# Score matmuls of a recurrence step issued two groups at a time in the first token half

## The chip, the cores and the metric

The kernel runs on one core of a Trainium2 chip. The metric is the device time of one execution in microseconds (us); lower is better. The engines have their own in-order instruction queues and meet only through semaphores: PE (TensorE, the matrix engine), DVE (VectorE), ACT (ScalarE), POOL (GpSimd) and SP (SyncE, which here only issues transfers).

## What is computed

The reference is one layer of a decoder block over 2048 tokens of 1024 features. After a norm and a modulation, one large projection gives the columns of four token mixers and of their gates. The mixer that matters here is the gated linear recurrence, worked in chunks:

```python
h = rmsnorm(x, g_pre[l]) * (1.0 + scale[:, None]) + shift[:, None]
p = h @ w_in[l]                      # 1024 x 8704, split into mixers and gates
...
def step(S, inp):                    # gated recurrence, 4 heads of 64
    qc, kc, vc, gc = inp
    b = jnp.cumsum(gc, axis=2)
    o_inter = jnp.einsum('bhtk,bhkv->bhtv', qc * jnp.exp(b), S)
    decay = jnp.exp(jnp.where(causal, diff, NEG))      # diff = b_t - b_s
    scores = jnp.einsum('bhtk,bhtsk,bhsk->bhts', qc, decay, kc)
    o = o_inter + jnp.einsum('bhts,bhsv->bhtv', scores, vc)
    S_new = (jnp.exp(b_last[:, :, 0, :])[..., None] * S
             + jnp.einsum('bhsk,bhsv->bhkv', kc * jnp.exp(b_last - b), vc))
```

The other mixers are a multi-window pooling, a short convolution and a differential attention. All are gated, projected, merged and projected once more; a norm and the residual end the layer.

## The kernel before, in words

The program has two stages. The first (`trunk`) computes the projection and all mixers; the second (`merge_and_output`) merges. The change touches `trunk` alone.

**Products and slots.** The projection is a row of 476 products, 238 for each half of the tokens (1024 tokens each). A product is 12 matmuls of 128x512 (four weight blocks, three split parts each: lines 1790 to 1792) into one of two PSUM banks `gb`, in turn. Seven products j = 0 to 6 make one unit of two columns of tiles. Every engine walks through the same loop over slots n = 0, 1, 2, ...: in slot n PE does product n, and each engine adds, by a table of slots, the small work of the mixers. So the place of a piece of work is set by the slot in which it is written.

**What holds a product.** Product n needs its bank free (`bank_free`): the result of product n-2 must have been taken out. For j = 0, 2, 3, 6 ScalarE copies it (`copy_out`, line 1013), for j = 1, 4, 5 VectorE adds it to another (`add_out`, line 1324, called "the sum" below). Both are done at the head of slot n+1 of their engine for product n. Product n also needs its split weights, made three slots ahead by ScalarE (`high`, line 990) and VectorE (`low`, line 1314); VectorE's part waits for ScalarE's.

**The recurrence's steps.** There are 16 steps of 128 tokens, 8 in each half. In the first half step i has its base at slot 130 + 12i, in the second at 372 + 25i/2. "Slot +k" below is the slot k behind the base of its step. A step has four score groups r = 0 to 3 (`rounds`): each is 8 small matmuls of 64 rows (lines 1928 and 1931; the profile has two records for each, so 16) into PSUM tile `score[r % 2]`. VectorE takes each group out with four predicated copies (`pick`, lines 1535 and 1540) into `AT`. Group r may start when the copies of group r-2 are done. The first two groups belong to one half of the heads, the last two to the other.

In the first half, before the change, PE has the groups at slots +0, +2, +4, +6 and VectorE its copies at +1, +3, +5, +7. In the second half the groups stand two at a time, at +0 and +4, and the copies at +1, +2, +5, +6.

**What else VectorE has in those slots** (the steps overlap: work at a negative offset is of the step that follows). In slot +2: after the sum and the weight split, `shares` of the next step (lines 1480 and 1481, which wait for ScalarE's `B_k_s`, line 1135) and `finish` of the step before (lines 1568, 1570, 1573). In slot +3: `queries` (line 1484). In slot +4: `scan` (1488, 1492, 1494). In slots +5 and +6: `distances_x` (1504). In slot +7: `decay_keys` (1511). Within one slot the copies of `pick` come behind the sum and the weight split and ahead of the rest. On PE, slot +0 has the norm matmul of the step before (1958), +4 the transposes (1966, 1967), +8 the outputs (1945 to 1952), all behind the groups of their slot.

Of the kernel before, what the change touches and what calls it, by code (L numbers as in the profile page):

```python
# [107 lines left out]
def kind(u):  # L108
    col = column(u)
    if col >= MIX_TILES or col < LOCAL_TILES:  # L110
        return "plain"
    return {20: "q", 24: "k", 28: "v", 32: "gate"}[col - col % 4]
# [51 lines left out]
def trunk(nc, x, c, w_ada, b_ada, g_pre, g_post, w_in, consts, diff_lam, diff_norm, hgrn_lb, hgrn_norm, conv_w, pool_w, pool_scale,  # L164
# [7 lines left out]
    with ExitStack() as ctx:  # L172
# [241 lines left out]
        def finished(half, s, lag):  # L414

            return ending.get(piece(half, s, lag))
# [12 lines left out]
        def mix_step(slot, offset):  # L429

            return MIX_BASE.index(slot - offset) if slot - offset in MIX_BASE else None

        MIX_HALF = NT // 2

        def step_in(half, slot, offset):

            i = mix_step(slot, offset)
            return i if i is not None and i // MIX_HALF == half else None

        def score_step(n, r):  # L440

            i = step_in(0, n, 2 * r)
            return step_in(1, n, (0, 0, 4, 4)[r]) if i is None else i

        def pick_step(n, r):

            i = step_in(0, n, 2 * r + 1)
            return step_in(1, n, (1, 2, 5, 6)[r]) if i is None else i

        def later(ap, level):  # L450

            return ap.rearrange("p (n u) -> p n u", u=2 * LEVELS[level])[:, :, LEVELS[level]:]

        def later_packed(ap, level):

            return ap[:, 0:P // 2].rearrange("p (n u) -> p n u", u=LEVELS[level])
# [846 lines left out]
        def _(dve):  # L1303
# [225 lines left out]
            def pick(i, r):  # L1529
                dve.wait_ge(r_done, 4 * i + r + 1)  # L1530
                for y in range(4):
                    level = 4 * (r % 2) + y
                    if level < NL - 1:
                        m = LEVELS[level]
                        ins = nc.vector.copy_predicated(
                            AT[:, r // 2, :, :].rearrange("p h (n u) -> p h n u", u=2 * m)[:, :, :, m:],
                            later(masks[:, level, :], level).unsqueeze(1).to_broadcast([P, 2, P // (2 * m), m]),
                            score[r % 2][:, :, y, 0:P // 2].rearrange("p h (n u) -> p h n u", u=m))
                    else:
                        ins = nc.vector.copy_predicated(AT[:, r // 2, :, :], masks[:, level, :].unsqueeze(1).to_broadcast([P, 2, P]),  # L1540
                                                        score[r % 2][:, :, y, :])
                    if y < 3:
                        link(ins)
                ins.then_inc(picked, 1)
                dve.wait_ge(picked, 4 * i + r + 1)
# [87 lines left out]
            for n in range(SLOTS):  # L1633
# [17 lines left out]
                for b, off in OUT_SLOT.items():  # L1651
                    v, r = divmod(n - off, PER)
# [44 lines left out]
                for half, s in att_slot(n):  # L1697
# [7 lines left out]
                    i = finished(half, s, GATE) if half else None  # L1705
# [7 lines left out]
                    if n == MIX_BASE[MIX_HALF * half] - 16:  # L1713
                        begin_mixers(half)
                for r in range(4):
                    i = pick_step(n, r)
                    if i is not None:
                        pick(i, r)
                i = mix_step(n, -10)
                if i is not None:  # L1720
                    shares(i)
                i = mix_step(n, -9)
                if i is not None:
                    queries(i)
                i = mix_step(n, -8)
                if i is not None:
                    scan(i)
                i = mix_step(n, -7)
                if i is not None:
                    distances_x(i, 0, 0, 3)  # L1730
                i = mix_step(n, -6)
                if i is not None:
                    distances_x(i, 0, 3, NL - 1)
                i = mix_step(n, -5)
                if i is not None:
                    decay_keys(i)
                i = mix_step(n, -4)
                if i is not None:
                    decay_first_queries(i)
                i = mix_step(n, -3)  # L1740
# [3 lines left out]
                i = mix_step(n, -2)  # L1744
                if i is not None:
                    distances_x(i, 1, 2, NL - 1)
                i = mix_step(n, 11)
                if i is not None:
                    advance_state(i)
                i = mix_step(n, 12)  # L1750
                if i is not None:
                    pool_out(i)
                i = mix_step(n, 14)
                if i is not None:
                    finish(i)
                i = mix_step(n, 1)
# [4 lines left out]
        def _(pe):  # L1761
# [15 lines left out]
            def product(n, part):  # L1777
                u, j = divmod(n, PER)
                if part == 0:
                    if made(n):  # L1780
                        pe.wait_ge(wlo, made_before(n) + 1)
                    else:
                        pe.wait_ge(w_kept[n % RING], 16 * (ring_uses(n) + 1))
                    if u % NU == 0:
                        operand_ready(u // NU, j)
                    bank_free(n)
                to, fresh = gb[n % 2][:, :], j in (0, 1, 3)
                hi, lo = w_hi[n % RING], w_lo[n % RING]
                for k in range(part * KH // 2, (part + 1) * KH // 2):
                    mm(to, hi[:, k, :], h_hi[j][:, k, :], start=(fresh and k == 0), stop=False, skip_group_check=True)  # L1790
                    mm(to, hi[:, k, :], h_lo[j][:, k, :], start=False, stop=False, skip_group_check=True)  # L1791
                    last = mm(to, lo[:, k, :], h_hi[j][:, k, :], start=False, stop=(k == KH - 1), skip_group_check=True)  # L1792
                if part:
                    last.then_inc(product_done, 1)
# [98 lines left out]
            def attention_ahead(half, s):  # L1893
                z = piece(half, s)
                if z is not None:
                    scores(z)
                i = finished(half, s, GATE) if half else None
                if i is not None:
                    turn_back(i)

            def attention_behind(half, s):
                z = piece(half, s, VALUES)
                if z is not None:
                    values(z)
                z = piece(half, s, TURN)
                if z is not None:
                    turn(z)
                i = None if half else finished(half, s, ON)
                if i is not None:
                    turn_back(i)  # L1910

            def rounds(i, r):
                if r == 0:
                    pe.wait_ge(prep0, 2 * i + 2)
                if r == 1:
                    pe.wait_ge(q_ready, i + 1)
                    pe.wait_ge(sig_ready, i + 1)
                if r == 2:
                    pe.wait_ge(prep1, 2 * i + 2)
                if 4 * i + r >= 2:  # L1920
                    pe.wait_ge(picked, 4 * i + r - 1)
                t = r // 2
                for y in range(4):
                    level = 4 * (r % 2) + y
                    for h in range(2):
                        rows_h = slice(64 * h, 64 * h + 64)
                        if level < NL - 1:
                            last = mm(later_packed(score[r % 2][:, h, y, :], level), X[rows_h, t, level, :],
                                      later(QX[rows_h, t, level, :], level), start=True, stop=True)
                        else:  # L1930
                            last = mm(score[r % 2][:, h, y, :], k_s[i % 2][rows_h, t, :], q_s[i % 2][rows_h, t, :], start=True, stop=True)
                last.then_inc(r_done, 1)
# [46 lines left out]
            for n in range(SLOTS):  # L1979
                for part in range(2):  # L1980
                    if n < PRODUCTS:
                        product(n, part)
                    if (n, part) in att_at:
                        attention_ahead(*att_at[n, part])
                    if (n, part) in att_behind:
                        attention_behind(*att_behind[n, part])
                if n == 0:
                    for q in range(12, 16):
                        turn_x(0, q)
                for b, off in OUT_SLOT.items():  # L1990
                    v, r = divmod(n - off, PER)
                    if r == 0 and 0 <= v < UNITS and kind(v) == "v":
                        turn_v(v, b)
                if 0 <= n - PREP - 9 < 16:
                    turn_x(1, n - PREP - 9)
                if n == PREP + 28:
                    sum_row()

                for r in range(4):
                    i = score_step(n, r)  # L2000
                    if i is not None:
                        rounds(i, r)
                i = mix_step(n, 8)
                if i is not None:
                    outputs(i)
                i = mix_step(n, 12)
                if i is not None:
                    norms(i)
                i = mix_step(n, 4)
                if i is not None:  # L2010
                    transposes(i)
# [418 lines left out]
```

## Time and profile before

| | us |
|---|---|
| median of 3 runs | 2371.06 |
| lowest, highest | 2364.52, 2377.28 |
| profiled execution | 2368.83 |
| its span, first to last instruction | 2367.0 |
| first-half recurrence steps, slots 130 to 225 | 560.85 to 911.43 |
| second-half recurrence steps | 1570.33 to about 1904 |

The profiled execution lies 2.2 us under the median of the runs. The span is cut into stages by what goes on beside the products. The steps that the change touches are all in the first of the two stretches named.

### The profile page before, as it was taken

What the parts mean: (1) busy time and instruction counts of PE and PEld (TensorE: products, weight loads), DVE (VectorE), ACT (ScalarE), POOL (GpSimd) and SP (SyncE); (2) the same over time, 40 slices, a digit from 0 to 9 for tenths busy, and PEclk for the clock granted to TensorE, in tenths of its full rate; (3) what the DMA queues carried; (4) which work ended last, traced back from release to release, by engine and by line L of the source; (5) the groups of instructions that cost most, each with busy time, mean ns of one, the idle gap of its engine ahead of it and who ended that gap; (6) DMA issues with size and microseconds to landing.
All of it is one profiled execution on the core that took longest, in us unless ns stands there. A gap on an engine that the chain in (4) does not pass through costs nothing. (4 is left out here: it accounts for less than half of the span.)

```text
span 2367.0 us, 35153 instructions
## 1 busy us (share of the span) xinstructions
PE 2228.6 (94%) x11573; PEld 1852.3 (78%) x11573; DVE 1452.9 (61%) x2649; ACT 1166.9 (49%) x2448; POOL 846.7 (36%) x747
## 2 busy tenths in 40 slices
PE   4798999999999999999999999999999968899998
PEld 3687788877777778787888888888888856787886
DVE  7765777748788785435776766444555435375571
ACT  5643566635465453444666565344535244444351
POOL 1222333326565661121222222123434216254452
PEclk7899999999999999999999999999999989999999
DMA  7878888778778778856666474588778766555561
GB/s 270 294 228 304 275 255 263 233 259 296 264 267 283 255 245 303 309 146 213 186 184 176 149 206 143 176 282 254 232 241 259 222 247 234 169 214 195 186 227 62
DMA packets 336940, 544.82 MB, mean 230 GB/s; under 512 B 26592, under 2 KB 216448, under 8 KB 331904
## 3 DMA queue, kind: packets, MB, share of 16 engines
q1 hardware_dynamic: 306528, 432.56, 54.6%
q10 hardware_dynamic: 30240, 110.11, 14.6%
q8 instruction: 91, 1.49, 0.3%
q14 instruction: 81, 0.66, 0.1%
HBM read 326.04 MB, written 221.77 MB: 231 GB/s over the span
## 5 line engine op out<-in xcount | busy, mean ns | idle before, releaser
L1790 PE MATMUL gb<-h_hi,w_both 128*128 128x512 f32 x1904 | 779.3, 409 | 53.6 <-ACT o L1013 28.1
L1792 PE MATMUL gb<-h_hi,w_both 128*128 128x512 f32 x1904 | 751.4, 395 | 0.0
L1791 PE MATMUL gb<-h_lo,w_both 128*128 128x512 f32 x1904 | 749.3, 394 | 0.0
L1790 PEld LDWEIGHTS gb<-h_hi,w_both 128*128 128x128 f32 x1904 | 362.2, 190 | 134.3 <-issue 64.4
L1792 PEld LDWEIGHTS gb<-h_hi,w_both 128*128 128x128 f32 x1904 | 361.2, 190 | 78.8
L1791 PEld LDWEIGHTS gb<-h_lo,w_both 128*128 128x128 f32 x1904 | 362.9, 191 | 66.1 <-issue 0.2
L1013 ACT ACTIVATE o<-gb 128x512 f32<-128x512 f32 x272 | 161.6, 594 | 342.6 <-PE gb L1792 296.0
L1078 ACT ACTIVATE C_prob<-C_sc,C_negm 128x512 f32<-128x512 f32 (+3 forms) x320 | 198.4, 622 | 222.3 <-DVE C_negm L1412 214.4
L881 POOL TENSOR_TENSOR C_prob<-C_prob,C_cf 128x512 f32<-128x512 f32 (+3 forms) x160 | 159.0, 1018 | 368.7 <-DVE C_cf L1434 364.0
L1324 DVE TENSOR_TENSOR o<-gb,o 128x512 f32<-128x512 f32 x204 | 140.2, 687 | 216.3 <-PE gb L1792 205.0
L1314 DVE TENSOR_TENSOR w_both<-w,w_both 128x512 fp32r<-128x512 f32 x190 | 171.1, 901 | 148.2 <-ACT w_both L990 148.1
L1412 DVE TENSOR_REDUCE C_negm<-C_sc 128x1 f32<-128x512 f32 (+3 forms) x320 | 179.6, 602 | 49.8 <-PE C_sc L1860 46.7
L862 POOL TENSOR_TENSOR s<-w 128x512 f32<-128x512 f32 x38 | 56.4, 1483 | 318.4 <-DMA w<-in_w_in_dram 301.0
L2330 PE MATMUL D_mb<-D_y_hi,D_wm_hi 128*128 128x512 f32 x320 | 128.8, 403 | 30.2 <-DVE D_wm_lo L2183 27.0
L990 ACT ACTIVATE w_both<-w 128x512 fp32r<-128x512 f32 x190 | 118.6, 625 | 70.8 <-PE gb L1792 61.1
L1885 PEld LDWEIGHTS C_ob<-C_v_tok,C_at 128*128 128x128 f32 x1088 | 144.0, 192 | 11.1 <-ACT C_at L1091 0.4
L1885 PE MATMUL C_ob<-C_v_tok,C_at 128*128 128x128 f32 x1088 | 147.6, 275 | 0.0
L1444 DVE SCALAR_TENSOR_TENSOR C_prob<-C_prob,C_cf 128x512 f32<-128x512 f32 (+3 forms) x160 | 133.9, 838 | 2.6 <-POOL C_prob L881 2.2
L2162 POOL TENSOR_TENSOR D_gate<-D_gate 128x1024 f32<-128x1024 f32 x32 | 76.9, 2403 | 149.6 <-DVE D_gate L2201 149.6
L2331 PE MATMUL D_mb<-D_y_lo,D_wm_hi 128*128 128x512 f32 x320 | 127.3, 398 | 0.0
L2332 PE MATMUL D_mb<-D_y_hi,D_wm_lo 128*128 128x512 f32 x320 | 126.9, 397 | 0.0
L1859 PE MATMUL C_sc<-C_ks,C_qt 128*128 128x512 f32 (+3 forms) x320 | 118.8, 371 | 5.3 <-ACT C_prob L1078 5.2
(236 smaller groups left out, 3730.3 us busy)
## 6 DMA issues: line engine op xcount, KB each, us to landing
wS_scratch<-w_both SPq DMA_DIRECT2D x210, 512.0 KB, 3.8
w_both<-wS_scratch ACTq DMA_DIRECT2D x210, 512.0 KB, 4.6
w<-in_w_in_dram SPq DMA_DIRECT2D x76, 512.0 KB, 5.2
gT_scratch<-o SPq DMA_DIRECT2D x128, 256.0 KB, 4.8
D_gate<-gT_scratch SPq DMA_DIRECT2D x32, 1024.0 KB, 4.9
pT_scratch<-o SPq DMA_DIRECT2D x80, 256.0 KB, 4.3
D_wm_stage<-wm_scratch SPq DMA_DIRECT2D x32, 640.0 KB, 6.1
C_qt<-qB_scratch SPq DMA_DIRECT2D x128, 128.0 KB, 3.5
```

The source lines that it names most:

```text
L881: tt(second, second, cf[i % 3][:, 1, p:p + 1].to_broadcast([P, width(z)]), ALU.mult).then_inc(scaled, 1)
L1013: a(o[b][:, :], gb[n % 2][:, :], ACT.Copy).then_inc(copied, 1)
L1078: a(prob[z % PROBS][:, m, 0:width(z)], sc[(2 * z + m) % 3][:, 0:width(z)], ACT.Exp, bias=negm[i % 2][:, m, p:p + 1], accum_out=sums[i % 2] ...
L1314: tt(w_lo[n % RING][:, :, :], source(n), w_hi[n % RING][:, :, :].bitcast(F32), ALU.subtract).then_inc(wlo, 1)
L1324: tt(o[b][:, :], gb[n % 2][:, :], o[c][:, :], ALU.add).then_inc(summed, 1)
L1412: nc.vector.tensor_reduce(negm[i % 2][:, m, p:p + 1], sc[(2 * z + m) % 3][:, 0:width(z)], AX.X, ALU.max, negate=True).then_inc(max_ready, 1)
L1444: stt(first_map, first_map, cf[i % 3][:, 0, p:p + 1], prob[z % PROBS][:, 1, 0:width(z)], ALU.mult, ALU.add).then_inc(a_ready, 1)
L1790: mm(to, hi[:, k, :], h_hi[j][:, k, :], start=(fresh and k == 0), stop=False, skip_group_check=True)
L1791: mm(to, hi[:, k, :], h_lo[j][:, k, :], start=False, stop=False, skip_group_check=True)
L1792: last = mm(to, lo[:, k, :], h_hi[j][:, k, :], start=False, stop=(k == KH - 1), skip_group_check=True)
L1885: last = mm(ob[i % 2][:, 0, :], at[z % 2][:, y, :], v_tok[:, 4 * p + y, :], start=(z == begin[i] and y == 0), stop=(p == 0 and y == nb - 1))
L2330: mm(mb[b][:, :], wm_hi[d % 2][:, k, :], y_hi[:, k, :], start=(k == c0), stop=False)
```

## The change

The groups and the copies of the first half take the slots that those of the second half have. PE issues groups 0 and 1 in slot +0 and groups 2 and 3 in slot +4; VectorE copies group 0 in +1, group 1 in +2 (it was +3), group 2 in +5 and group 3 in +6 (it was +7). The second half is as it was. Three helper functions go; nothing is added or removed in the work itself.

```diff
-        def step_in(half, slot, offset):
-            i = mix_step(slot, offset)
-            return i if i is not None and i // MIX_HALF == half else None
-        def score_step(n, r):
-            i = step_in(0, n, 2 * r)
-            return step_in(1, n, (0, 0, 4, 4)[r]) if i is None else i
-        def pick_step(n, r):
-            i = step_in(0, n, 2 * r + 1)
-            return step_in(1, n, (1, 2, 5, 6)[r]) if i is None else i
...
                 for r in range(4):
-                    i = pick_step(n, r)
+                    i = mix_step(n, (1, 2, 5, 6)[r])
                     if i is not None:
                         pick(i, r)
...
-                for r in range(4):
-                    i = score_step(n, r)
+                for first in (0, 2):
+                    i = mix_step(n, 2 * first)
                     if i is not None:
-                        rounds(i, r)
+                        rounds(i, first)
+                        rounds(i, first + 1)
```

The change moves the lines of the file up by 15 behind this place (L1314 before is L1299 after). PE at the base of step 0, before: the second group (`B_score1`) stands two products behind the first.

```order
L1792 MATMUL gb0<-h_hi4,w_both2 128x512
L1928 MATMUL B_score0<-B_QX,B_X 128x64 x8
L1790 MATMUL gb1<-h_hi5,w_both3 128x512
...
L1792 MATMUL gb0<-h_hi6,w_both0 128x512
L1928 MATMUL B_score1<-B_QX,B_X 128x64 x6
L1931 MATMUL B_score1<-B_q_s0,B_k_s0 128x128 x2
L1790 MATMUL gb1<-h_hi0,w_both1 128x512
```

The same place after:

```order
L1777 MATMUL gb0<-h_hi4,w_both2 128x512
L1913 MATMUL B_score0<-B_QX,B_X 128x64 x8
L1913 MATMUL B_score1<-B_QX,B_X 128x64 x6
L1916 MATMUL B_score1<-B_q_s0,B_k_s0 128x128 x2
L1775 MATMUL gb1<-h_hi5,w_both3 128x512
```

The second group has moved up to the first, ahead of two products.

VectorE in slots +2 and +3 of step 1, before; the row `o<-gb,o` is the sum that opens slot +3:

```order
L1314 TENSOR_TENSOR w_both<-w,w_both 128x512
L1480 TENSOR_SCALAR B_f_ab<-B_f_s 128x256
L1481 TENSOR_SCALAR B_f_ab<-B_f_s 128x256
L1568 TENSOR_TENSOR B_sgate<-B_sgate,B_g_in 128x256
L1570 TENSOR_TENSOR B_rs<-B_b,B_rs 128x256
L1573 SCALAR_TENSOR_TENSOR B_yh<-B_rs,norm_h,B_sgate 128x256
L1324 TENSOR_TENSOR o<-gb,o 128x512
L1314 TENSOR_TENSOR w_both<-w_1,w_both 128x512
L1535 COPY_PREDICATED B_AT<-B_masks,B_score 128x32x4
L1535 COPY_PREDICATED B_AT<-B_masks,B_score 128x64x2
L1535 COPY_PREDICATED B_AT<-B_masks,B_score 128x128
L1540 COPY_PREDICATED B_AT<-B_masks,B_score 128x256
```

The same place after:

```order
L1299 TENSOR_TENSOR w_both<-w,w_both 128x512
L1520 COPY_PREDICATED B_AT<-B_masks,B_score 128x32x4
L1520 COPY_PREDICATED B_AT<-B_masks,B_score 128x64x2
L1520 COPY_PREDICATED B_AT<-B_masks,B_score 128x128
L1525 COPY_PREDICATED B_AT<-B_masks,B_score 128x256
L1465 TENSOR_SCALAR B_f_ab<-B_f_s 128x256
L1466 TENSOR_SCALAR B_f_ab<-B_f_s 128x256
L1553 TENSOR_TENSOR B_sgate<-B_sgate,B_g_in 128x256
L1555 TENSOR_TENSOR B_rs<-B_b,B_rs 128x256
L1558 SCALAR_TENSOR_TENSOR B_yh<-B_rs,norm_h,B_sgate 128x256
L1309 TENSOR_TENSOR o<-gb,o 128x512
```

The copies of group 1 have moved ahead of `shares`, `finish` and the sum. In slots +6 and +7 it is the same with group 3: its copies now stand ahead of the distances (line 1504) and of the sum that opens slot +7, where that slot has one.

## Rows read from the trace of the kernel before

**Rows 1.** The page: busy time of an engine, share of the span, instructions.
```profile
PE 2228.6 (94%) x11573; PEld 1852.3 (78%) x11573; DVE 1452.9 (61%) x2649; ACT 1166.9 (49%) x2448; POOL 846.7 (36%) x747
```

**Rows 2.** Waits of PE, 560 to 960 us: total us, times, longest.
```profile
PE gb L1790 <- DVE o L1324: 12.8, 10, 2.5
PE gb L1790 <- ACT o L1013: 6.9, 5, 3.3
```

**Rows 3.** Timeline of PE, first step 7: start us, us, engine, line, operation, tiles.
```profile
870.34 0.39 PE L1790 MATMUL gb<-h_hi,w_both 128*128 128x512 f32 x1
...
884.22 0.39 PE L1790 MATMUL gb<-h_hi,w_both 128*128 128x512 f32 x1
...
888.48 0.48 PE L1790 MATMUL gb<-h_hi,w_both 128*128 128x512 f32 x1
...
898.06 0.39 PE L1790 MATMUL gb<-h_hi,w_both 128*128 128x512 f32 x1
...
911.43 0.39 PE L1790 MATMUL gb<-h_hi,w_both 128*128 128x512 f32 x1
```

**Rows 4.** Timeline of PE, a second-half step of 12 slots, groups two at a time.
```profile
1693.72 0.39 PE L1790 MATMUL gb<-h_hi,w_both 128*128 128x512 f32 x1
...
1707.23 0.39 PE L1790 MATMUL gb<-h_hi,w_both 128*128 128x512 f32 x1
...
1712.44 0.47 PE L1790 MATMUL gb<-h_hi,w_both 128*128 128x512 f32 x1
...
1720.70 0.39 PE L1790 MATMUL gb<-h_hi,w_both 128*128 128x512 f32 x1
...
1734.07 0.39 PE L1790 MATMUL gb<-h_hi,w_both 128*128 128x512 f32 x1
```

**Rows 5.** Timeline of PE, steps 1 to 6; in brackets idle us and releaser.
```profile
619.04 0.47 PE L1790 MATMUL gb<-h_hi,w_both 128*128 128x512 f32 x1 [1.82 <-DVE o L1324]
...
624.97 0.48 PE L1790 MATMUL gb<-h_hi,w_both 128*128 128x512 f32 x1
...
721.23 0.39 PE L1790 MATMUL gb<-h_hi,w_both 128*128 128x512 f32 x1
...
749.52 0.47 PE L1790 MATMUL gb<-h_hi,w_both 128*128 128x512 f32 x1 [0.87 <-DVE o L1324]
...
799.02 0.47 PE L1790 MATMUL gb<-h_hi,w_both 128*128 128x512 f32 x1 [2.48 <-DVE o L1324]
...
802.46 0.47 PE L1790 MATMUL gb<-h_hi,w_both 128*128 128x512 f32 x1 [0.46 <-DVE o L1324]
...
841.39 0.47 PE L1790 MATMUL gb<-h_hi,w_both 128*128 128x512 f32 x1 [2.35 <-DVE o L1324]
```

**Rows 6.** Timeline of DVE, step 1, slots +1 to +3.
```profile
606.35 2.00 DVE L1314 TENSOR_TENSOR w_both<-w,w_both 128x512 fp32r<-128x512 f32 x1
...
614.63 0.69 DVE L1314 TENSOR_TENSOR w_both<-w,w_both 128x512 fp32r<-128x512 f32 x1 [4.60 <-ACT w_both L990]
615.99 0.29 DVE L1480 TENSOR_SCALAR B_f_ab<-B_f_s 128x256 f32<-128x256 f32 x1 [0.66 <-ACT B_k_s L1135]
...
618.21 0.68 DVE L1324 TENSOR_TENSOR o<-gb,o 128x512 f32<-128x512 f32 x1
...
619.41 1.25 DVE L1535 COPY_PREDICATED B_AT<-B_masks,B_score 128x128 f32<-128x128 uint8 x3
620.70 0.45 DVE L1540 COPY_PREDICATED B_AT<-B_masks,B_score 128x256 f32<-128x256 uint8 x1
621.19 1.10 DVE L1484 TENSOR_TENSOR B_q_s<-B_q_s,B_in 128x256 f32<-128x256 f32 x1
```

**Rows 7.** Timeline of DVE, step 3: the sum that opens slot +7.
```profile
719.79 0.68 DVE L1324 TENSOR_TENSOR o<-gb,o 128x512 f32<-128x512 f32 x1
```

**Rows 8.** Windows: stretch, length, busy us (count) of PE, PEld, DVE, ACT, POOL, then PE's granted clock, transfer share, GB/s.
```profile
620.00:623.60 3.60, 3.60 (x11) 2.33 (x10) 3.50 (x7) 0.63 (x1) 3.44 (x4) 0.53 0.55 218
799.00:802.40 3.40, 2.97 (x12) 2.17 (x12) 3.33 (x6) 0.67 (x3) 2.71 (x3) 1.00 0.59 231
```

## The prediction

> **What bounds the kernel now.** I read the page first. PE is busy for 94% of the span and no other engine for more than 61% [rows 1], so time is saved only where PE's own row gets shorter or where PE stands still. Next the waits of PE between 560 and 960 us, the stretch with the first half's steps: PE stands for 12.8 us behind VectorE's sums and for 6.9 us behind ScalarE's copies [rows 2]. Then PE's timeline, slot by slot, in three kinds of steps. Step 7 of the first half has no wait at all; its 12 slots take 911.43 - 870.34 = 41.09 us [rows 3]. A step of the second half, which already has the groups two at a time and also no wait, takes 1734.07 - 1693.72 = 40.35 us for 12 slots [rows 4]. The other first-half steps are held somewhere, and rows 5 shows where: nearly always at slot +4 to +6, for a sum of VectorE. Last the timeline of VectorE in step 1, to see why the sum is late [rows 6]: VectorE stood for 4.60 us behind ScalarE, then for 0.66 us behind ScalarE's `B_k_s`, and had five operations to do before the sum at 618.21; PE went on at 619.04, 0.83 us behind the start of the sum.
>
> **Part 1: fewer interruptions of the products.** Each of the 8 steps has four groups before and two pairs after; the matmuls are the same. The two steps without a wait price it: 40.35 - 41.09 = -0.74 us for a step [rows 3, 4]. That is all on PE, the path that sets the end. If PE is never held it makes 8 x -0.74 = -5.9 us. The saving isn't evenly spread. The slot with a pair is longer: slot +4 takes 888.48 - 884.22 = 4.26 us before and 1712.44 - 1707.23 = 5.21 after, +0.95. Two groups later it is won back: from the start of slot +4 to that of +8 it is 13.84 us before and 13.47 after, -0.37; from the start of +5 to that of +8 it is 9.58 and 8.26, -1.32 [rows 3, 4]. The first pair gives the other -0.37. So it matters where a step is held: whatever comes before the last wait is lost in that wait.
>
> **Part 2: copies ahead of a sum.** The copies of one odd group hold VectorE from 619.41 to 621.19, 1.78 us [rows 6]. They move from slot +3 to +2 and from +7 to +6. Where the slot they leave opens with a sum, that sum is now behind them. By the index of the product (j = 1, 4 or 5) this is so in slot +3 of steps 1, 4 and 6 and in slot +7 of steps 1, 3 and 6: six places of sixteen. Elsewhere they stand between the same two sums as before, and no sum gets later.
>
> In slot +3 of steps 1, 4 and 6 PE is already waiting for just this sum: it goes on at 619.04, 749.52 and 841.39 [rows 5]. The scores are there long before, since PE made them in slot +0. VectorE's 0.66 us of standing ahead of `shares` is filled by the copies. So each of the three sums comes about 1.78 - 0.66, less 0.1 of overlap at the edges, = 1.0 us later, and PE with it. The bounds of one such place are 0 (if ScalarE comes yet later) and 1.78.
>
> In slot +7 VectorE has more room. In step 3 the sum starts at 719.79 [rows 7], so PE could have gone on at 719.79 + 0.83 = 720.62, and came at 721.23 [rows 5]: 0.61 us of slack. After, the sum is 1.78 - 0.66 (the filled wait in slot +2; I take it to be the same in step 3) = 1.12 later, and PE 0.5 later. For step 6 I take 1.0 (bounds 0 and 1.78), because the pair in slot +4 also comes later there and the copies find nothing to fill. In step 1 I take 0: its last slots start late enough on PE.
>
> **Part 3: step by step.** Step 7, no wait: -0.74. Step 0, held before slot +4 only: keeps the second half, -0.37. Step 2, held a little at +6: between -0.37 and -1.32, I take -0.7. Step 5, held at +5 and +6 by sums that don't get later [799.02 and 802.46 in rows 5]: the longer slot +4 vanishes in the wait, -1.32 stay, and the filled idle time of VectorE gives some 0.2 more: -1.5. Step 1: +1.0 - 0.37 = +0.6. Step 4: the same, +0.6. Step 3: +0.5. Step 6: +1.0 - 0.37 + 1.0 = +1.6. The sum is 0.0 us: the gain of part 1 is eaten by part 2.
>
> **Part 4: PE's clock.** After the wait that ended at 619.04 the granted clock fell to about half (mean 0.53 from 620.0 to 623.6 [rows 8]), that is to 1.2 of 2.4 GHz; after the one of 2.48 us that ended at 799.02 it stayed at 1.00 [rows 5, 8]. Where it fell, slot +4 took 624.97 - 619.04 = 5.93 us for 4.26: 1.67 us. Two waits grow past 2 us or appear anew: in slot +4 of step 4 (0.87 in its row, and PE both comes 0.38 earlier and is let go 1.0 later) and in slot +8 of step 3. A fall costs 0 to 1.67 each; at 3 in 5 the two make +2.0 us. The Trainium skill ("TensorE: Matmul & The Clock Gate", "Why this matters for your kernels") advises against idle gaps between bursts of matmuls because the clock falls behind them. The waits here bear that out in one case and not in the other, so I take neither 0 nor the whole.
>
> **The sum.** 0.0 + 2.0 = +2 us against the profiled execution (2368.83 to 2370.8). That execution lies 2.2 us under the median of the runs; on the median it is 2371.06 + 2 = **2373 us**. Each of the six places can be off by about 1 us and the clock by 2, so this case by itself spans 2368 to 2378. Outside the first half's steps nothing is reordered on any engine, and the products behind them run without slack, so the difference reaches the end unchanged.
>
> **The rivals.**
>
> *Only the interruptions count.* The second half has these very slots and no wait at all [rows 4]. If VectorE is let go earlier in the first half too, because its waits for ScalarE shrink as PE's slots +1 and +2 come later, the six places cost nothing: -5.9 us, 2365.2 us. Against it: in the first half VectorE also splits weights, and PE waits for it 10 times [rows 2]. Chance 0.22.
>
> *Collisions with GpSimd.* The split of a weight takes 0.69 us in one row and 2.00 in another of the same shape [rows 6]; in the second case GpSimd was at work. Moving the copies shifts `finish` and the splits against GpSimd's convolution in slot +2. If one split in every second step changes from the short to the long form, that is 4 x 1.31 = +5.2 us on top of the forecast, 2378.2 us; the other way round it would be as much less. The Trainium skill ("SBUF — State Buffer", "Terms") says that VectorE and GpSimd arbitrate for a shared pair of ports, which one holds for a whole instruction while the other is blocked. The rows agree in kind, since the predicated copies have near equal times everywhere and the splits have not. Chance 0.12 for a clear change of the slower kind.
>
> *Every moved copy costs its full time: slower.* The place is slot +3 and +7 in the six cases. The 0.66 us aren't filled, because ScalarE is itself held back by the later sums, and the slack at +7 is gone since the pair in slot +4 comes 0.95 later: 6 x 1.78 = +10.7, less 8 x 0.37 = 3.0 of the saving, and four falls of the clock, 4 x 1.67 = +6.7: +14.4, 2385.5 us. It decides from the point where PE waits at slot +8 in all three steps with a sum there. Against it: in step 3 there was 0.61 us of slack, and VectorE idles for some us in slots +8 to +10 of most steps. Chance 0.08.
>
> That the change does nothing can be left out: the instructions do stand in the new order.
>
> **How the numbers follow.** Forecast 0.58 (2373, from 2368 to 2378), only interruptions 0.22 (2365), collisions 0.12 (2378), full price 0.08 (2385.5). The range leaves out the last and the far side of the spread of runs, whose own extent was 2364.5 to 2377.3: 2363 to 2381. A measurement of this kernel can tell some 0.5% from no change, which is 11.9 us. Only the full price reaches beyond that on the slow side, 0.08; on the fast side it would take twice the gain of part 1, 0.02. The rest, 0.90, is no difference that can be told.
>
> **What would show it.** In the profile after, a first-half step without waits should take 40.35 us on PE; if it doesn't, part 1 is wrong. PE's waits behind the sums should grow from 12.8 to about 17 us in the same stretch, with the resumption in slot +4 of steps 1, 4 and 6 later against the base of the step by 1.0 us, a new wait at slot +8 of steps 3 and 6, and a shorter one at +5 of step 5. ScalarE's share of the waits should stay near 6.9 us or grow by a few tenths. The row of the copies should still have about 1.78 us for four. The forecast is wrong if VectorE's total of the splits (line 1314) changes by over 4 us, or if the stage behind 911 us takes a different time from before.

## The result and the profile after

Over 20 runs of each the changed kernel takes 2373.88 us (2370.2 to 2376.41) and the kernel before 2369.0 us (2363.32 to 2377.28): ratio 1.002, 95% interval 1.0014 to 1.0027. It is slower by 4.9 us (3.3 to 6.4), less than the 0.5% that the prediction took for the least that can be told, and yet outside the noise of 20 runs. The forecast was a change of +2 us and a time of 2373. The time came nearer than the change because 2373 was built on the median of three runs of the kernel before, 2371.06, which lies 2.1 us above the median of twenty; that is luck. The profiled execution took 2373.97 us, its span is 2372.2.

The page after: PE's own busy time hardly moved (2225.0 us for 2228.6); the matrix engine has no more work, it stands longer.

```profile
span 2372.2 us, 35153 instructions
PE 2225.0 (94%) x11573; PEld 1851.0 (78%) x11573; DVE 1456.1 (61%) x2649; ACT 1166.8 (49%) x2448; POOL 850.9 (36%) x747
```

The waits of PE between 560 and 960 us, against [rows 2]:

```profile
PE gb L1775 <- DVE o L1309: 16.3, 9, 4.5
PE gb L1775 <- ACT o L998: 6.8, 5, 3.3
PE B_b L1943 <- DVE S L1539: 2.4, 1, 2.4
```

The sums of VectorE hold PE for 3.5 us more, near the 17 us forecast; ScalarE's copies are where they were (6.9 before); the third row is new in this size. Before, the norm matmul waited 0.3 us once in the stretch.

The step without waits is what the second half promised. PE's timeline of step 7, slots +0, +4 and +12, against [rows 3]:

```profile
875.27 0.39 PE L1775 MATMUL gb<-h_hi,w_both 128*128 128x512 f32 x1
...
888.78 0.39 PE L1775 MATMUL gb<-h_hi,w_both 128*128 128x512 f32 x1
...
915.62 0.39 PE L1775 MATMUL gb<-h_hi,w_both 128*128 128x512 f32 x1
```

It takes 915.62 - 875.27 = 40.35 us for 41.09, to the hundredth the -0.74 of the forecast. The steps with waits, PE's timeline again, against [rows 5]:

```profile
621.43 0.47 PE L1775 MATMUL gb<-h_hi,w_both 128*128 128x512 f32 x1 [4.49 <-DVE o L1309]
...
700.43 1.19 PE L1943 MATMUL B_b<-B_osq,B_mean_w 128*128 128x256 f32 x2 [2.38 <-DVE S L1539]
...
725.04 0.47 PE L1775 MATMUL gb<-h_hi,w_both 128*128 128x512 f32 x1 [0.71 <-DVE o L1309]
...
754.14 0.47 PE L1775 MATMUL gb<-h_hi,w_both 128*128 128x512 f32 x1 [1.93 <-DVE o L1309]
...
761.05 0.48 PE L1775 MATMUL gb<-h_hi,w_both 128*128 128x512 f32 x1
...
846.46 0.47 PE L1775 MATMUL gb<-h_hi,w_both 128*128 128x512 f32 x1 [3.87 <-DVE o L1309]
```

With the starts of the products read off that timeline, every step can be set beside its forecast:

| step | before, us | after, us | difference | forecast |
|---|---|---|---|---|
| 0 | 41.43 | 41.28 | -0.15 | -0.37 |
| 1 | 47.16 | 48.96 | +1.80 | +0.6 |
| 2 | 41.99 | 41.68 | -0.31 | -0.7 |
| 3 | 43.17 | 45.36 | +2.19 | +0.5, clock to come |
| 4 | 42.25 | 44.14 | +1.89 | +0.6, clock to come |
| 5 | 47.48 | 45.17 | -2.31 | -1.5 |
| 6 | 46.01 | 47.42 | +1.41 | +1.6 |
| 7 | 41.09 | 40.35 | -0.74 | -0.74 |
| sum | 350.58 | 354.35 | +3.77 | 0.0, and +2.0 for the clock |

So 3.8 of the 5.2 us by which the spans of the two profiled executions differ lie in this stretch. The other 1.4 lie in parts that are the same in both kernels: 0.4 ahead of the stretch, and 1.0 behind it, from its end to the end of the span (1456.6 us for 1455.6). In the other kernels below that same last part takes 1454.4 to 1458.9 us, so a difference of a microsecond or two between two profiled executions says nothing by itself.

**Why the sum in step 1 is later than forecast.** VectorE in slots +2 and +3 of step 1, to be read against [rows 6]:

```profile
614.34 1.03 DVE L1299 TENSOR_TENSOR w_both<-w,w_both 128x512 fp32r<-128x512 f32 x1 [3.58 <-ACT w_both L975]
615.30 1.25 DVE L1520 COPY_PREDICATED B_AT<-B_masks,B_score 128x128 f32<-128x128 uint8 x3
616.58 0.44 DVE L1525 COPY_PREDICATED B_AT<-B_masks,B_score 128x256 f32<-128x256 uint8 x1
617.06 0.51 DVE L1465 TENSOR_SCALAR B_f_ab<-B_f_s 128x256 f32<-128x256 f32 x1
617.50 0.28 DVE L1466 TENSOR_SCALAR B_f_ab<-B_f_s 128x256 f32<-128x256 f32 x1
617.70 0.90 DVE L1553 TENSOR_TENSOR B_sgate<-B_sgate,B_g_in 128x256 f32<-128x256 f32 x1
618.63 0.43 DVE L1555 TENSOR_TENSOR B_rs<-B_b,B_rs 128x256 f32<-128x256 f32 x1
619.09 1.59 DVE L1558 SCALAR_TENSOR_TENSOR B_yh<-B_rs,norm_h,B_sgate 128x256 f32<-128x256 f32 x1
620.60 0.68 DVE L1309 TENSOR_TENSOR o<-gb,o 128x512 f32<-128x512 f32 x1
```

The copies are there and take 617.06 - 615.30 = 1.76 us, as costed; the 0.66 us of standing is filled, as costed, and `shares` starts 0.8 us later against the base of the step than before. But `finish` behind them has an operation of 1.59 us, and before it was one of 0.48:

```profile
617.81 0.48 DVE L1573 SCALAR_TENSOR_TENSOR B_yh<-B_rs,norm_h,B_sgate 128x256 f32<-128x256 f32 x1
```

That row is of the kernel before. The 1.59 us, from 619.09, cover a whole weight operation of GpSimd (1.26 us from 619.14); the operation of 0.90 us stands beside the end of GpSimd's convolution. Before, the convolution ran beside `finish` too, and the weight operation only began at 618.84, behind it. The copies had pushed `finish` onto it.

**The same place in steps 4 and 6.** There `shares` starts 1.0 us later as well (12.48 us behind the base of step 4 for 11.45, 14.55 in step 6 for 13.51). What follows differs: in step 4 the operations up to the sum happened to be 0.3 us shorter than before, in step 6 they were 0.5 us longer. One operation of `shares` took 0.29 us for 0.86, but the other, with a single tensor as input (`L1481` before, 0.28 us), met a weight operation of GpSimd (VectorE's timeline, then GpSimd's):

```profile
842.61 1.35 DVE L1466 TENSOR_SCALAR B_f_ab<-B_f_s 128x256 f32<-128x256 f32 x1
```

```profile
842.43 1.39 POOL L847 TENSOR_TENSOR s<-w 128x512 f32<-128x512 f32 x1 [0.35 <-DMA w<-in_w_in_dram]
```

So the three sums are 2.1, 0.7 and 1.5 us later: the copies give about 1.0 each time, and the meetings with GpSimd add to it or take from it.

**Why step 3 lost 2.2 us.** Not where the forecast looked. The state update (of step 2) of slot +11 (line 1539, two operations) and GpSimd in the same microseconds, after:

```profile
695.88 4.41 DVE L1539 SCALAR_TENSOR_TENSOR S<-S,B_eb,B_rs 128x128 f32<-128x128 f32 x2
```

```profile
695.92 2.08 POOL L913 TENSOR_TENSOR B_QX<-B_X,B_q_s 128x896 f32<-128x896 f32 x1 [0.96 <-ACT B_X L1145]
698.07 2.07 POOL L916 TENSOR_TENSOR B_X<-B_X,B_k_s 128x896 f32<-128x896 f32 x1
```

And before:

```profile
693.22 0.62 DVE L1554 SCALAR_TENSOR_TENSOR S<-S,B_eb,B_rs 128x128 f32<-128x128 f32 x2
```

4.41 us for 0.62, each of the two about as long as one of GpSimd's products. The norm matmul in slot +0 is written to wait for the state update (`state_done`), so PE stood 2.38 us until 700.43, and the clock fell.

**The clock.** Windows of PE's granted clock (last but two of the columns) in the changed kernel, four behind the waits that ended at 621.43, 700.43, 754.14 and 846.46, and one behind a wait of 1.80 us that ended at 795.43:

```profile
621.80:625.20 3.40, 3.40 (x10) 2.62 (x9) 3.37 (x6) 0.00 (x0) 3.10 (x3) 0.50 0.81 310
700.30:703.70 3.40, 3.27 (x8) 2.63 (x9) 3.38 (x7) 3.35 (x7) 2.07 (x2) 0.50 0.40 159
755.00:758.30 3.30, 3.30 (x10) 2.52 (x8) 3.27 (x4) 0.00 (x0) 2.62 (x3) 0.50 0.88 338
847.10:850.50 3.40, 3.40 (x10) 2.63 (x9) 2.40 (x6) 0.00 (x0) 0.00 (x0) 0.50 0.66 252
795.50:798.90 3.40, 3.40 (x15) 2.83 (x16) 2.92 (x7) 2.67 (x7) 3.10 (x5) 1.00 0.57 208
```

It fell to its lower level in four places of the eight steps, for two before. In step 4, slot +4 then took 761.05 - 754.14 = 6.91 us for 5.21, +1.70. In step 3, slots +0 and +1 took 12.09 us for the 8.07 of a step without waits; less the wait of 2.38 that leaves 1.64 for the clock. The two falls more are 3.3 of the 3.8 us of the stretch.

### The profile page after: what moved, and what is told of

Its sections match the earlier page's. It is cut to its first block and busy times, and to the rows that moved or that the text cites. A ratio compares the mean times of both kernels' runs of the same rounds, so it can differ in the third digit from the quotient of the medians.

```text
span 2372.2 us, 35153 instructions
## 1 busy us (share of the span) xinstructions
PE 2225.0 (94%) x11573; PEld 1851.0 (78%) x11573; DVE 1456.1 (61%) x2649; ACT 1166.8 (49%) x2448; POOL 850.9 (36%) x747
## 5 line engine op out<-in xcount | busy, mean ns | idle before, releaser
L1299 DVE TENSOR_TENSOR w_both<-w,w_both 128x512 fp32r<-128x512 f32 x190 | 166.6, 877 | 148.7 <-ACT w_both L975 148.4
```

The lines of the kernel that those rows point to most:

```text
L1299: tt(w_lo[n % RING][:, :, :], source(n), w_hi[n % RING][:, :, :].bitcast(F32), ALU.subtract).then_inc(wlo, 1)
```

## The experiments

The kernels of the table below are the kernel before with other slot tables for the first half. A row gives PE's slots of the four groups, then VectorE's slots of their copies. The two lines of `score_step` and `pick_step` that read them are the only edit, here for the third row:

```diff
-            i = step_in(0, n, 2 * r)
+            i = step_in(0, n, (0, 0, 4, 4)[r])
...
-            i = step_in(0, n, 2 * r + 1)
+            i = step_in(0, n, (1, 3, 5, 7)[r])
```

| kernel | groups on PE | copies on VectorE | ratio to before | interval |
|---|---|---|---|---|
| before | 0, 2, 4, 6 | 1, 3, 5, 7 | 1 | |
| the changed kernel | 0, 0, 4, 4 | 1, 2, 5, 6 | 1.0020 | 1.0014 to 1.0027 |
| pairs, copies as before | 0, 0, 4, 4 | 1, 3, 5, 7 | 0.9966 | 0.9955 to 0.9977 |
| pairs, group 1 moved | 0, 0, 4, 4 | 1, 2, 5, 7 | 0.9997 | 0.9985 to 1.001 |
| pairs, group 3 moved | 0, 0, 4, 4 | 1, 3, 5, 6 | 1.0008 | 0.9995 to 1.0021 |
| first pair only | 0, 0, 4, 6 | 1, 2, 5, 7 | 1.0013 | 1.0001 to 1.0024 |
| second pair only | 0, 2, 4, 4 | 1, 3, 5, 6 | 0.9997 | 0.9987 to 1.0008 |

**Pairs on PE, the copies left alone.**

> PE issues the score groups in pairs at +0 and +4 in the first half, as in the changed kernel, but VectorE keeps its copies at +1, +3, +5, +7, as before. My theory (the loss is that the odd group's copies stand ahead of a sum): no sum gets later, the 0.74 us of a step comes through, about 5 us faster than the kernel before (8 x 0.74 = 5.9, less the parts of steps 1, 4 and 6 that lie ahead of their waits, plus 0.9 that step 5 hides); ratio about 0.998. Rival (the longer slots +0 and +4 of PE are themselves what delays VectorE and ScalarE): slower than before by as much as the changed kernel, about 4.9 us, ratio 1.002.

Measured: 2361.75 us, ratio 0.9966 (0.9955 to 0.9977), 8 us faster than the kernel before by the ratio, 7.1 by the medians. The rival falls: PE's longer slots harm nothing worth naming. What the change does to PE is a gain, and what it does to VectorE's queue costs more than that gain. Its waits of PE in the eight steps:

```profile
PE gb L1790 <- DVE o L1324: 10.4, 8, 2.5
PE gb L1790 <- ACT o L1013: 4.5, 4, 2.7
PE B_score L1928 <- DVE B_AT L1540: 0.8, 2, 0.6
```

The third row is the price of leaving the copies late: group 3 in slot +4 twice waited for the copies of group 1, 0.8 us in all. The gain is larger than the 5 us expected; the interval reaches from 5.4 to 10.7 us, so it holds the -5.9 us of the prediction's part 1. The profiled execution is 4.4 us shorter, 4.0 of them in the eight steps, with three falls of the clock there for two. Where the rest of the 8 us comes from no trace shows.

**One pair at a time.**

> Only groups 0 and 1 are paired (PE at +0, +0, +4, +6; copies at +1, +2, +5, +7): the copies of group 1 stand ahead of the sum of slot +3 in steps 1, 4 and 6. My theory, with the sizes of the changed kernel's trace (sums of slot +3 later by 2.1, 0.7 and 1.6 us, one more fall of the clock at 1.7, the other five steps at -0.37): about 4 us slower than before, ratio 1.0017, so most of the loss. Rival (both pairs cost alike): about 2.5 us slower, ratio 1.001.

Measured: ratio 1.0013 (1.0001 to 1.0024), 3 us slower. That fits the theory's 4 us and the rival's 2.5 alike.

> Only groups 2 and 3 are paired (PE at +0, +2, +4, +4; copies at +1, +3, +5, +6): the copies of group 3 stand ahead of the sum of slot +7 in steps 1, 3 and 6, where VectorE has slack. My theory: 8 x -0.37 = -3.0, about -0.9 more in step 5, where the longer slot +4 lies under a wait, and +1 to +1.5 for steps 3 and 6: about 2.5 us faster than before, ratio 0.999. Rival (both pairs cost alike): 2.5 us slower, ratio 1.001.

Measured: ratio 0.9997 (0.9987 to 1.0008), no difference. The interval holds the 0.999 that I expected, near its edge, and leaves out the rival's 1.001 by as little, so this run decides little. Its trace shows a cost of group 3's copies that I had not counted: the norm matmul of step 3 waits 3.3 us for the state update here too.

**One group's copies at a time, under the same pairs.**

> Pairs on PE as in the changed kernel; only the copies of group 1 are moved (+1, +2, +5, +7), those of group 3 stay at +7. Two places of one theory are told apart: by the trace of the changed kernel, the copies of group 3 at +6 delay ScalarE's decays at +7, its weight copies and VectorE behind them, so that in step 3 the state update meets GpSimd's long products and the norm matmul waits 2.4 us, and they make the new waits at +8. Without them: 5 us less than the changed kernel, so about the kernel before, ratio 0.9995 to 1.0005. If the whole loss comes from the sums of slot +3, the ratio stays at 1.001 to 1.002.

> Pairs on PE; only the copies of group 3 are moved (+1, +3, +5, +6). If the two moves add up from the pairs with the copies as before (8 us faster than the kernel before): 4 to 5 us of it are lost to the late state update and the waits at +8, so 3 to 4 us faster than before, ratio 0.9985. If group 3's copies cost nothing: ratio 0.9966, as the pairs with the copies as before.

Measured: 0.9997 (0.9985 to 1.001) with group 1 moved and 1.0008 (0.9995 to 1.0021) with group 3 moved. The first came as expected, the second did not: I expected 0.9985, and moving group 3's copies alone loses 10 us against 0.9966, twice what I had put down. Group 1's move alone loses 7 us. Both together lose 13 us (0.9966 to 1.0020); the 17 of the parts can't be told from that, with intervals of 1.5 to 3 us on either side of each ratio. These sizes rest on the medians alone: the eight steps of the profiled executions take 346.60 us with the copies as before, 346.01 with group 1 moved (the second fastest of that kernel's 12 runs was profiled) and 349.87 with group 3 moved, so the traces show none of the 7 us and 3.3 of the 10. In the profile of the kernel with group 3 moved the wait of step 3 is back, to the hundredth:

```profile
693.22 1.19 PE L1958 MATMUL B_b<-B_osq,B_mean_w 128*128 128x256 f32 x2 [2.38 <-DVE S L1554]
```

and its waits of PE in the eight steps:

```profile
PE gb L1790 <- DVE o L1324: 11.5, 8, 2.3
PE gb L1790 <- ACT o L1013: 4.1, 3, 3.1
PE B_b L1958 <- DVE S L1554: 2.4, 1, 2.4
```

It stands in the four traces of full kernels in which group 3's copies are at +6 ahead of the distances in step 2, and in none of those that have them at +7. How it comes about can be read in the step before. VectorE and ScalarE in slots +6 and +7 of step 2, the kernel with group 3 moved:

```profile
671.89 0.90 DVE L1504 TENSOR_TENSOR B_X<-B_b_s 128x128 f32<-128x128 f32 x4
...
675.79 0.69 DVE L1314 TENSOR_TENSOR w_both<-s,w_both 128x512 fp32r<-128x512 f32 x1 [2.07 <-ACT w_both L990]
```

```profile
672.82 0.95 ACT L1159 ACTIVATE B_X<-B_X 128x896 f32<-128x896 f32 x1 [2.59 <-DVE B_X L1504]
673.81 0.96 ACT L1160 ACTIVATE B_X<-B_X 128x896 f32<-128x896 f32 x1
674.67 0.58 ACT L1013 ACTIVATE o<-gb 128x512 f32<-128x512 f32 x1
675.14 0.62 ACT L990 ACTIVATE w_both<-s 128x512 fp32r<-128x512 f32 x1
```

The copies stand ahead of the four distance operations; ScalarE's two long decays wait 2.59 us for those; its copy of a product and of a weight queue behind the decays; VectorE's split waits 2.07 us for that weight, and all of this is 1.5 us later against the base of the step than in the kernel with the copies as before. From there the lateness is GpSimd's: two of its short operations meet VectorE (0.91 us for 0.61 and 1.05 for 0.28, at 678.09 and 679.05), and its weight operations come about 1.5 us later, while VectorE, which then waits 1.30 us for ScalarE instead of 3.03, is back at its old place. So VectorE's next split meets a weight operation, and the state update, 0.8 us late by that, meets the products. VectorE and GpSimd, slot +11 and behind, the same kernel:

```profile
686.50 1.78 DVE L1314 TENSOR_TENSOR w_both<-w,w_both 128x512 fp32r<-128x512 f32 x1
...
688.65 4.42 DVE L1554 SCALAR_TENSOR_TENSOR S<-S,B_eb,B_rs 128x128 f32<-128x128 f32 x2
```

```profile
686.30 1.43 POOL L869 TENSOR_TENSOR s<-w 128x512 f32<-128x512 f32 x1
```

With the copies as before that split takes 0.68 us and the two state updates 0.61, and the update is done 0.5 us before GpSimd's first product begins.

**The same copies behind the distances.** The edit leaves them in slot +6, but the last in it:

```diff
-                    if i is not None:
+                    if i is not None and not (r == 3 and i < MIX_HALF):
                         pick(i, r)
...
                     distances_x(i, 0, 3, NL - 1)
+                i = step_in(0, n, 6)
+                if i is not None:
+                    pick(i, 3)
```

> As the pairs with copies at +1, +3, +5, +6, but in slot +6 the copies of group 3 stand behind the four distance operations instead of ahead of them; the sum that opens slot +7 is behind them in both. Theory (group 3's copies cost because the distances are what ScalarE waits for at +7, and its weight copies and VectorE's splits queue behind that): ScalarE's decays start as early as before, the norm matmul of step 3 does not wait 2.4 us for the state, and the time comes back to 0.997 to 0.9985 of the kernel before. Rival (they cost because the sum of slot +7 is behind them, steps 1, 3 and 6): nothing changes from 1.0008.

Measured: ratio 0.9998 (0.9988 to 1.0008). In the trace (ScalarE's timeline, then VectorE's) the chain is broken as the theory says: ScalarE's decays wait 1.01 us, the state update takes 0.61 us, and the norm matmul doesn't wait.

```profile
675.83 0.96 ACT L1159 ACTIVATE B_X<-B_X 128x896 f32<-128x896 f32 x1 [1.01 <-DVE B_X L1504]
```

```profile
692.38 0.61 DVE L1554 SCALAR_TENSOR_TENSOR S<-S,B_eb,B_rs 128x128 f32<-128x128 f32 x2
```

Step 3 takes 42.24 us for 46.25, the eight steps together 344.65 for 349.87. The median, though, came down by 2.4 us only (1.0008 to 0.9998, intervals that overlap), not by the 5 of the stage and not to the 0.9985 expected; by its time alone the rival, no change from 1.0008, isn't excluded. The 5 us of the stage also hold the clock, which fell once there for three times in the other, and new waits: 1.91 us in slot +4 of step 5, for the copies of group 1 (0.29 in the other), and 0.86 in slot +8 of step 6. In its profiled execution PE enters the stage at 563.4 us, for 558.5 in the other, in a part of the program that is the same in both. So the chain is shown, and its full price isn't.

**GpSimd's share in the loss.** Seven of the nine operations of `conv_part` in slot +2 go, from both kernels:

```diff
-                link(tt(acc[:, :, :], z_s[:, :, 2:], w[2], ALU.mult))
...
-                link(tt(acc[:, :, :], acc[:, :, :], c_in[:, 2:4, HALO_C:], ALU.mult))
                 pool.wait_ge(sigc_ready, i + 1)
-                link(tt(s_cg[:, :, :], s_cg[:, :, :], c_in[:, 6:8, HALO_C:], ALU.mult))
-                tt(yc[:, :, :], acc[:, :, :], s_cg[:, :, :], ALU.mult).then_inc(yc_ready, 1)
+                tt(yc[:, :, :], z_s[:, :, 2:], s_cg[:, :, :], ALU.mult).then_inc(yc_ready, 1)
```

> The kernel before with most of the short convolution left out on GpSimd: 2 of its 9 operations in slot +2 stay (one product, one gate), so the convolution branch is not computed in full. Prices GpSimd's collisions with VectorE in slots +2 and +3. Theory: VectorE's two-input operations there take the short form and the weight copies of ScalarE wait less for GpSimd; the first-half steps lose 3 to 6 us of their waits, ratio 0.998.

> The changed kernel with the same part of the convolution left out on GpSimd. If about half of the lateness of the sums at +3 (2.1 us in step 1, of which 1.0 are the copies and 1.1 longer operations beside GpSimd) comes from the collisions, the sum in step 1 is only 1.0 us later than in the short-convolution form of the kernel before, and the two differ by 2 to 3 us rather than 4.9. If the collisions play no part, they differ by 4.9 us as the full kernels do.

Measured: 0.9973 (0.9957 to 0.9989) and 0.9985 (0.9974 to 0.9997) of the full kernel before. The two differ by 3 us, where the full ones differ by 4.9; the intervals overlap, so this alone is weak. The timeline of step 1 is sharper. Start of the step and the product let go in slot +4, the form of the kernel before:

```profile
601.16 0.39 PE L1783 MATMUL gb<-h_hi,w_both 128*128 128x512 f32 x1
...
617.45 0.47 PE L1783 MATMUL gb<-h_hi,w_both 128*128 128x512 f32 x1 [1.31 <-DVE o L1317]
```

and of the changed kernel:

```profile
601.61 0.39 PE L1783 MATMUL gb<-h_hi,w_both 128*128 128x512 f32 x1
...
618.88 0.72 PE L1783 MATMUL gb<-h_hi,w_both 128*128 128x512 f32 x1 [2.37 <-DVE o L1317]
```

16.29 and 17.27 us: the sum is 0.98 us later. In the full kernels it is 2.1 later (16.76 and 18.89). So in step 1 the forecast's 1.0 us is the cost of the copies by themselves, and the other 1.1 us come from meeting GpSimd, whose convolution is mostly gone here and whose weight operation comes earlier (10.3 us behind the base of the step for 16.6). The other two steps don't repeat it: the sum of step 4 is 0.02 us later between the short forms (0.7 in the full kernels), because an operation of `shares` takes 1.32 us in the short form of the kernel before, and that of step 6 is 1.7 us later (1.5), since `shares` still meets a weight operation there (1.35 us). The short form of the changed kernel also has no wait of the norm matmul in step 3, though its copies of group 3 stand ahead of the distances and VectorE's split waits 2.07 us for its weight there too: the state update, 1.6 us earlier against the base, comes clear of GpSimd's products. Whether the late copies cost those 2.4 us hangs on where GpSimd is at that moment.

**Copies fitted to the sums.** Each step gets the slots where no sum stands behind:

```diff
-            i = step_in(0, n, 2 * r + 1)
+            for k in (1, 2, 5, 6, 7):
+                i = step_in(0, n, k)
+                if i is not None and k == (1, 2 if i in (0, 2, 7) else 1, 5, 7 if i in (1, 3, 6) else 6)[r]:
+                    return i
...
```

> Pairs on PE as in the changed kernel, and each step's odd copies where no sum stands right behind them: group 1 at +1 in steps 1, 3, 4, 5, 6 (VectorE stands for ScalarE there) and +2 in steps 0, 2, 7; group 3 at +7 in steps 1, 3, 6 and at +6 elsewhere. My theory: no sum later, so about 5 to 6 us faster than before, ratio 0.9975 to 0.998, and at least as fast as pairs with the copies as before. Rival (PE's longer slots are the cause): about 4.9 us slower, ratio 1.002.

Measured: 0.9982 (0.997 to 0.9993), faster than before, a little less so than the 0.9975 to 0.998 expected. I had also said that it would be at least as fast as the plain version with the copies left alone, and it isn't: its median is 3.8 us longer (2365.53 for 2361.75). It looked only at sums. Step 2 has its copies of group 3 at +6, ahead of the distances, and the norm matmul of step 3 waited 2.4 us again. The last kernel takes that out, with group 3 at +7 in all steps:

> Pairs on PE, the copies of group 1 at +1 in steps 1, 3, 4, 5, 6 and at +2 in steps 0, 2, 7, those of group 3 always at +7. If group 3's copies at +6 are what held copies_fitted back, the norm matmul of step 3 no longer waits and the stage of the eight steps takes 339 to 341 us for 350.6 before: 9 to 11 us faster than before, ratio 0.9955 to 0.996. If copies_fitted was held back by group 1's copies at +1, it stays at 0.998.

Measured: 2357.72 us, ratio 0.9954 (0.9939 to 0.9969), 11 us faster than the kernel before. The norm matmul of step 3 doesn't wait, as expected; the eight steps take 342.45 us in the profile, a little over the 339 to 341 expected. These are only 6 runs. It is the fastest of the kernels here, by its median; its interval overlaps that of the pairs with the copies as before (0.9955 to 0.9977), so the worth of fitting group 1 isn't settled.

## Why the prediction was right, and where it was off

**Part 1, fewer interruptions: right.** -0.74 us in the step without waits, as the two steps without waits of the kernel before had priced it. The runs put the whole PE side, with the copies left alone, at -8 us (-5.4 to -10.7), for -5.9 in the working. The profiled executions show 4.0 of it in the eight steps.

**Part 2, copies ahead of a sum: the right mechanism, a term left out.** The sums at +3 of steps 1, 4 and 6 are later against the base of their step by 2.1, 0.7 and 1.5 us, where each was put at 1.0. The 1.0 was the cost of the copies alone: what stands right behind them starts 0.8, 1.0 and 1.0 us later, and without most of the convolution the sum of step 1 came 0.98 later. What was left out is what follows, `shares` and `finish`, whose operations ran beside other work of GpSimd than before: 1.3 us longer in step 1, 0.3 shorter in step 4, 0.5 longer in step 6. The working took their durations as fixed.

**Part 2, the copies of group 3: wrong in place.** The forecast looked at the sum at +7 and at PE's slot +8 in steps 1, 3 and 6. There the changed kernel has one wait of 0.71 us, in step 3, and none in the others. The cost came by another way: distances late, ScalarE's decays late, weight late, GpSimd and VectorE shifted against each other, state update onto GpSimd's products, norm matmul late, all from copies in a slot (+6 of step 2) for which the forecast had said "Elsewhere they stand between the same two sums as before, and no sum gets later." No sum did. ScalarE waits for other operations of VectorE too.

**Part 3, steps 0, 2, 5 and 6** came within about 0.8 us of what was put down, step 6 by luck: it was to lose 1.0 at slot +3 and 1.0 at slot +7, and lost 1.5 and nothing. In step 5 the wait of 2.48 us at +5 went altogether, and the step gained 2.3 us for the 1.5.

**Part 4, the clock: the right number of falls, too cheap.** Two more falls in the stage, as said, but each cost all of its 1.7 us: 3.3 for the 2.0. One is in step 4, as said; the other came at the norm matmul of step 3, at +0 and not at +8. Without the two the stage is 0.4 us longer, for the 0.0 of the forecast; the misses in the single steps cancel in that sum. Of the five longest waits in the steps of this trace (1.80 us and more) four were followed by a fall, where the forecast took 3 in 5. The length of the waits alone doesn't give the number of falls: with group 1 moved by itself none followed a wait of 3.25 us in step 1. So stages of two traces can differ by the 1.7 of a fall that their waits don't explain.

**The rivals.** *Only the interruptions count* is the kernel with the copies left alone, so its mechanism is real, but not that of this change: VectorE wasn't let go earlier. *Collisions with GpSimd* was given 0.12 and is a good part of what happened: about 1.1 us in step 1 and the 2.4 us of step 3. The sign that the prediction named for being wrong, a change of over 4 us in VectorE's total of the weight splits, did come, and in the other direction: they got shorter by 4.8 us in the stretch from 560 to 965 us (100.8 for 105.6), while the state updates there went from 7.6 to 11.4 and the distances from 40.2 to 43.8. The collisions moved from one kind of operation to others that PE waits for. The other sign, a different time behind the eight steps, stayed away: 1.0 us, inside the spread of that part among the kernels here. *Full price* did not come.

## What to carry to other kernels

Take a change that moves work on two engines apart into its halves before judging it: here one half was worth about -8 us, the other about +13, and together they looked like a small loss. When work is moved up in an in-order queue, count every operation that it now precedes, not only the one that the bottleneck waits for. Ask of each who waits for it (here ScalarE for the distances), and which long operations of a neighbour on the same memory port it will then meet.

## What the runs showed of the hardware

A VectorE operation on SBUF can take several times its length beside GpSimd: two state updates took 4.41 us together for 0.62, while GpSimd's two products of 2.08 and 2.07 us ran, the last operation of `finish` 1.59 for 0.48, and an operation of `shares`, with one tensor as input, 1.35 for 0.28. The predicated copies, whose scores come from PSUM, kept their 1.25 and 0.44 us in the same slots. This agrees with the Trainium skill ("SBUF — State Buffer", "Terms"), by which the two engines arbitrate for one pair of ports and the loser is blocked, not slowed. It was known from the rows of the kernel before that a split can take 2.00 us for 0.69; not expected was that shifting a queue by 1.8 us moves such a collision onto an operation that PE waits for, five slots on.

The granted clock fell to 1.2 GHz behind waits of 1.93, 2.38, 3.87 and 4.49 us in the changed kernel and not behind one of 1.80; in the kernel before it fell behind one of 1.82 and not behind one of 2.48. With group 1 alone moved it did not fall behind one of 3.25 (PE's timeline, then the window with the granted clock of 1.00):

```profile
617.14 0.47 PE L1790 MATMUL gb<-h_hi,w_both 128*128 128x512 f32 x1 [3.25 <-DVE o L1324]
```

```profile
617.20:620.60 3.40, 3.40 (x22) 2.63 (x22) 3.40 (x4) 1.08 (x2) 3.32 (x3) 1.00 0.72 270
```

The length of a wait alone does not tell.
